# Probabilities scaled and turned by halves stream through the values, two query tiles at a time

## The chip, the cores and the metric

One core of one Trainium2 chip runs the program. The metric is device time in microseconds, the median of the runs of one kernel; lower is better. The engines are TensorE (PE, with its weight loads PEld), VectorE (DVE), ScalarE (ACT), GpSimd (POOL) and SyncE (SP, which issues DMAs).

## The reference

512 tokens of width 1024 pass a first block (a gated delta rule with its MLP) and then a second one, which mixes two kinds of attention. Only the second block's attention is touched:

```
q, k, v from h @ w_in_2        # 8 heads of width 64 over 2 groups of keys and values
p = masked_softmax(q k^T)      # two branches: selected keys and window; causal here
o = gate * (p @ v)             # summed over three branches for each head (the third reads blocks of keys)
o_mla = softmax(q' k'^T) @ v'  # 8 more heads, keys and values made from a latent
y = concat(o, o_mla) * silu(z) @ w_out_2
```

All is in float32, and the output must be close to a float32 reference.

## The kernel before, in words

Activations and weights of the large products are split into two parts, a rounded one and the rest (`hhi`, `hlo`, `whi`, `wlo`, type fp32r), and each product is made of three fp32r products: hi with hi, lo with hi, hi with lo (L2272). A small product is a plain float32 matmul, which the trace shows as two instructions of TensorE.

The attention of the second block is a spine of 96 steps, `for i in range(N_STEPS + 3)`, written out in the same order on every engine. Steps 0 to 63 are the sixteen pairs of head and branch of the two groups ("nsa"), steps 64 to 95 the 8 latent heads ("mla"); four steps are one head, one for each query tile of 128 tokens, and step i has (i % 4 + 1) * 128 keys. A step's work goes through the engines like this, with its line in the profile:

- PE `scores` (L3037): one float32 product into one of two PSUM banks.
- DVE `most`: the causal mask is added in PSUM (L2060), the row maximum is taken (L2062) and negated (L2064).
- ACT `soft` (L1138): the exponential into `prob`, with its row sum; two buffers.
- PE `turned`, two steps later (L3045): i % 4 + 1 transposes of `prob` into PSUM bank 4.
- ACT `turned` (L1146): the copy of bank 4 into `probT`, two buffers.
- PE `values`, three steps later (L3059): for each key tile `probT` is the weight (128x128) and `v`, 64 columns, moves. The output is tokens by 64.
- DVE `weigh` (L2070, L2076): the reciprocal of the row sum, times the gate. DVE `combine` (L2093, L2097): the output is scaled by it and added into `o_nsa` or written into `o_mla`, tokens by head width.

Between these PE runs six (five in three of four steps from 32 to 63, none in 68 to 71) of the 512-column products of the projections (`fill`), so that PE always has work. Other jobs sit at fixed steps (`jobs(i)` on each engine): rotations, the third branch's windows and softmax (steps 9 to 44), latent projections (54 to 85). On ACT `spine_units(i)` runs first in a step. At 16 steps (4, 8, ... 32, 37, 41, 46, 51, 55, 60, 64, 68) it copies the finished unit out of PSUM and splits the next weights into `whi` (L1050); POOL then makes `wlo` (L1358). At the end of the nsa steps PE turns `o_nsa` back (`turn_mixed`, L2887, steps 69 and 70), DVE multiplies it with the gate `zs2` (`mix`, L2033), ACT and POOL split it, and the output projection can start (step 72). `o_mla` is turned at steps 75, 83 and 91 and at the end (L3068).

The order on each engine is that of the code; semaphores count finished steps. On DVE a step is `most(i)`, `weigh(i-1)`, `combine(i-3)`, `jobs(i)`.

## Time and profile before

| | |
|---|---|
| three runs, median | 1089.87 us (1088.97 to 1091.43) |
| the profiled execution | 1092.04 us, span 1090.2 us |
| granted TensorE clock | 0.995 of full speed |
| PE busy | 1064.6 us, 98% |
| DVE, ACT, POOL busy | 56%, 43%, 44% |
| attention spine | from 751.4 us to about 1070 us of the span |

A line of the page names the source line, the engine, the operation, output and inputs, how many there were, the busy time and the mean of one, and then how long the engine stood idle before them and who released it. In the timeline the first two columns are start and duration. Matmul durations overlap: the distance from one start to the next is what one costs.

### The profile page before, as it was taken

Reading aid. Unit: us, or ns where it says so; the run is one execution under the profiler, and the core shown is the slowest. Engines: PE = TensorE matmul, PEld = TensorE weight load, DVE = VectorE, ACT = ScalarE, POOL = GpSimd, SP = SyncE. Lnnn points to the kernel's source line nnn. Section 1 sums busy time; section 2 is a strip of 40 time slices with the busy share of each in tenths; the row PEclk is TensorE's granted clock in tenths of the full one; section 3 lists DMA queues with packets and bytes.
Section 4 is the critical chain, followed back from the end, with each engine's and each line's share of the span. In section 5 each row is a group of like instructions: output and inputs, shape, how many; then the busy total and the mean of one; then the engine's idle time right before and its main releaser. Section 6 shows DMA issues by size and latency. Waiting matters only on the chain. (4 is left out here: it accounts for less than half of the span.)

```text
span 1090.2 us, 16275 instructions
## 1 busy us (share of the span) xinstructions
PE 1064.6 (98%) x5659; PEld 878.4 (81%) x5659; DVE 611.7 (56%) x1365; ACT 473.7 (43%) x1057; POOL 483.9 (44%) x276
## 2 busy tenths in 40 slices
PE   7999999999999999999999999999999999999997
PEld 6888888888878888888888888877788887766775
DVE  6777747767646646512122126436956767644677
ACT  6654346566543431531331333343334444454544
POOL 5786413332436775774574575346222122113230
PEclk9999999999999999999999999999999999999999
DMA  6554431221106154354343543514112011000011
GB/s 214 145 136 130 109 97 49 78 58 50 56 25 209 49 174 156 96 174 135 116 154 102 149 154 97 150 27 110 40 39 68 21 39 49 20 20 11 20 69 78
DMA packets 167157, 100.08 MB, mean 92 GB/s; under 512 B 30424, under 2 KB 160812, under 8 KB 166060
## 3 DMA queue, kind: packets, MB, share of 16 engines
q1 hardware_dynamic: 166924, 99.06, 31.3%
q8 instruction: 43, 0.70, 0.3%
q14 instruction: 30, 0.25, 0.1%
q10 hardware_dynamic: 160, 0.07, 0.0%
HBM read 95.69 MB, written 3.16 MB: 91 GB/s over the span
## 5 line engine op out<-in xcount | busy, mean ns | idle before, releaser
L1260 POOL TENSOR_TENSOR wlo<-stage,whi 128x1024 fp32r<-128x1024 f32 (+1 forms) x105 | 274.5, 2618 | 215.8 <-ACT whi L763 215.4
L2272 PE MATMUL ps<-hhi,whi 128*128 128x512 f32 (+1 forms) x728 | 306.9, 422 | 1.9 <-DVE gated L2033 0.9
L2272 PE MATMUL ps<-hhi,wlo 128*128 128x512 f32 (+1 forms) x728 | 296.7, 408 | 0.0
L2272 PE MATMUL ps<-hlo,whi 128*128 128x512 f32 (+1 forms) x728 | 288.5, 400 | 0.0
L2272 PEld LDWEIGHTS ps<-hhi,whi 128*128 128x128 f32 (+1 forms) x728 | 137.0, 188 | 36.1 <-issue 5.4
L1358 POOL TENSOR_TENSOR wlo<-stage,whi 128x1024 fp32r<-128x1024 f32 (+3 forms) x40 | 73.3, 1835 | 205.5 <-ACT whi L1050 205.5
L763 ACT ACTIVATE whi<-stage 128x1024 fp32r<-128x1024 f32 x104 | 109.7, 1056 | 120.7 <-PE ps L2272 88.8
L2272 PEld LDWEIGHTS ps<-hhi,wlo 128*128 128x128 f32 (+1 forms) x728 | 137.2, 188 | 30.1 <-issue 6.6
L2272 PEld LDWEIGHTS ps<-hlo,whi 128*128 128x128 f32 (+1 forms) x728 | 137.1, 188 | 26.2 <-issue 1.9
L2272 PE MATMUL ps<-ahi,whi 128*128 128x512 f32 x312 | 124.1, 398 | 3.4 <-POOL alo L1310 3.4
L1138 ACT ACTIVATE prob<-ps,aneg 128x128 f32<-128x128 f32 (+1 forms) x96 | 50.7, 528 | 168.8 <-DVE aneg L2064 122.9
L2272 PE MATMUL ps<-alo,whi 128*128 128x512 f32 x312 | 122.2, 392 | 0.0
L2272 PE MATMUL ps<-ahi,wlo 128*128 128x512 f32 x312 | 122.2, 392 | 0.0
L1790 DVE TENSOR_TENSOR hf<-relu 128x512 f32<-128x512 f32 x32 | 27.8, 867 | 112.1 <-ACT relu L1026 108.4
L1796 DVE TENSOR_TENSOR xT<-xT,ps 128x512 f32<-128x512 f32 x32 | 22.0, 688 | 102.7 <-PE ps L2272 102.7
L2272 PEld LDWEIGHTS ps<-ahi,whi 128*128 128x128 f32 x312 | 58.7, 188 | 15.0 <-POOL alo L1310 3.9
L2272 PEld LDWEIGHTS ps<-alo,whi 128*128 128x128 f32 x312 | 58.6, 188 | 11.8
L2272 PEld LDWEIGHTS ps<-ahi,wlo 128*128 128x128 f32 x312 | 58.7, 188 | 10.9
L1485 DVE SCALAR_TENSOR_TENSOR acc<-ps,convw,acc 128x511 f32<-128x511 f32 (+2 forms) x72 | 53.6, 745 | 10.2 <-ACT acc L796 8.6
L1026 ACT ACTIVATE relu<-ps 128x512 f32<-128x512 f32 x32 | 19.1, 598 | 92.4 <-PE ps L2272 92.4
L3059 PEld LDWEIGHTS ps<-v,probT 128*128 128x128 f32 x320 | 45.6, 191 | 4.4
L1340 POOL TENSOR_TENSOR alo<-hf,ahi 128x512 fp32r<-128x512 f32 x32 | 45.3, 1416 | 8.5 <-ACT ahi L1020 8.5
(399 smaller groups left out, 1765.2 us busy)
## 6 DMA issues: line engine op xcount, KB each, us to landing
stage<-dn_w_in SPq DMA_DIRECT2D x32, 512.0 KB, 4.2
stage<-mlp_w_up SPq DMA_DIRECT2D x32, 512.0 KB, 4.6
stage<-mlp_w_down SPq DMA_DIRECT2D x32, 512.0 KB, 4.6
mod_w<-ada_w SPq DMA_DIRECT2D x8, 1536.0 KB, 6.6
stage<-w_in SPq DMA_DIRECT2D x17, 512.0 KB, 3.6
gcrow<-gc_rows SPq DMA_DIRECT2D x16, 256.0 KB, 3.7
stage<-dn_w_out SPq DMA_DIRECT2D x8, 512.0 KB, 3.4
stage<-w_in SPq DMA_DIRECT2D x9, 256.0 KB, 3.0
```

The costliest lines, as they stand in the source:

```text
L763: act.activation(whi[:, slot, 0:ks, 0:cols], stage[:, slot, 0:ks, 0:cols], ACT.Copy).then_inc(s["w_hi"], 1)
L1026: act.activation(relu[:, m % 2], up_bank(q, m), ACT.Relu).then_inc(s["mlp_relu"], 1)
L1138: act.activation(prob[:, i % 2, 0:keys], ps[:, 2 + i % 2, 0:keys], ACT.Exp, scale=SCALE if kind == "nsa" else SCALE_M, bias=aneg[:, i % 2: ...
L1260: pool.tensor_tensor(wlo[:, slot, 0:ks, 0:cols], stage[:, slot, 0:ks, 0:cols], whi[:, slot, 0:ks, 0:cols], ALU.subtract).then_inc(s["w_lo" ...
L1340: pool.tensor_tensor(alo[0][:, m], af[:, m % 2], ahi[0][:, m], ALU.subtract).then_inc(s["mlp_lo"], 1)
L1358: pool.tensor_tensor(wlo[:, n % RING, 0:ks, 0:cols], stage[:, n % RING, 0:ks, 0:cols], whi[:, n % RING, 0:ks, 0:cols], ALU.subtract).then_ ...
L1485: dve.scalar_tensor_tensor(out=a[:, t:T], in0=u[:, 0:T - t], scalar=convw[:, (3 - t) * 3 + seq, h:h + 1], in1=a[:, t:T], op0=ALU.mult, op1 ...
L1790: dve.tensor_tensor(af[:, m % 2], relu[:, m % 2], relu[:, m % 2], ALU.mult).then_inc(s["mlp_f"], 1)
L1796: dve.tensor_tensor(xT[:, m], xT[:, m], ps[:, (U_MLP + m) % 2, :], ALU.add).then_inc(s["res"], 1)
L2272: mm = pe.matmul(bank, w[:, slot, k - ks[0], 0:width], x[:, k], start=(i == 0), stop=(i == len(todo) - 1))
L3059: mm = pe.matmul(ps[:, value_bank(i), 0:DK], probT[:, i % 2, c * P:(c + 1) * P], v, start=(c == 0), stop=(c == qt))
```

## The change

`prob` is scaled before it is turned. ACT multiplies the reciprocal with the gate (`scaled`, one column) and then `prob` with the result, in place, one step after the exponential. PE turns it as before. ACT copies the turned block into an fp32r tile (the high part, `hi_even` or `probT`), and DVE writes the difference between PSUM and that copy into a second one (`turned_low`, the low part). The values are held as weights: 64 columns of high part and 64 of low part side by side (`vst`, `v_mla`). `values(p)` now runs once for two query tiles, at even steps: for each key tile that both need one product of 256 moving columns, and one of 128 columns for the last key tile, first for the high part of the probabilities, then for the low part. The output has 128 partitions (64 for each half of the values) and lies turned: head width by tokens. For nsa, both branches and all four tiles of a head add up in bank 7, and DVE adds the two halves to `o_nsa` once in eight steps; for mla it combines each pair. The turns of the mixed outputs go away. The third branch's values and the latent values are made in the layout that this needs; the latent values come in eight jobs (steps 63 to 66 and 78 to 81) instead of four. DVE now starts a step with `weigh(i-1)` and `turned_low(i-3)`, ahead of `most(i)`. Two bfloat16 constants that nothing read are gone.

```diff
         def step_key(i):
             if i < N_NSA:
-                return "nsa", i // 16, i // 8 % 2, i // 4 % 2, i % 4
+                return "nsa", i // 16, i // 4 % 2, i // 8 % 2, i % 4
...
+            def scaled(i):
+                kind, e, b, g, qt = step_key(i)
+                keys, coef = (qt + 1) * P, ainv[:, i % 4:i % 4 + 1]
+                act.wait_ge(s["at_inv"], i + 1)
+                if kind == "nsa":
...
+                    act.activation(coef, ainv[:, i % 4:i % 4 + 1], ACT.Copy, scale=gate2[:, qt, at:at + 1]).then_inc(s["at_coef"], 1)
+                    act.wait_ge(s["at_coef"], i + 1)
+                act.activation(prob[:, i % 2, 0:keys], prob[:, i % 2, 0:keys], ACT.Copy, scale=coef).then_inc(s["at_scale"], 1)
+
             def turned(i):
-                keys = (i % 4 + 1) * P
                 act.wait_ge(s["at_t"], i + 1)
-                if i >= 2:
-                    act.wait_ge(s["at_o"], i - 1)
-                act.activation(probT[:, i % 2, 0:keys], ps[:, 4, 0:keys], ACT.Copy).then_inc(s["at_tev"], 1)
+                if i >= 4:
+                    act.wait_ge(s["at_o"], i // 2 - 1)
+                act.activation(turned_tile(0, i), ps[:, 4, 0:(i % 4 + 1) * P], ACT.Copy).then_inc(s["at_tev"], 1)
...
             for i in range(N_STEPS + 2):
                 if i < N_STEPS:
                     spine_units(i)
+                if 1 <= i <= N_STEPS:
+                    scaled(i - 1)
+                if i < N_STEPS:
                     soft(i)
...
-            turned_rows(0, "vs")
             rotated("ks", kz[0], None)
+            value_low(0, "vs")
...
-            def mix(k, bank):
-                after(dve, "pe", f"turned {k}")
+            def mix(k):
+                dve.wait_ge(s["at_done"], combined(N_NSA // 2 - 1 if k < 4 else N_NSA // 2 + 4 * (k - 3) - 1))
                 if k >= 2:
                     after(dve, "pool", f"mix low {k - 2}")
-                done(dve.scalar_tensor_tensor(out=gated[:, k % 2], in0=bank, scalar=0.5, in1=zs2[:, k],
+                done(dve.scalar_tensor_tensor(out=gated[:, k % 2], in0=out_tile(k), scalar=0.5, in1=zs2[:, k],
...
+            def turned_low(i):
+                dve.wait_ge(s["at_tev"], i + 1)
+                dve.tensor_tensor(turned_tile(1, i), ps[:, 4, 0:(i % 4 + 1) * P], turned_tile(0, i), ALU.subtract).then_inc(s["at_lo"], 1)
+
+            def combine(p):
+                kind, e, b, g, x = pair_key(p)
+                if kind == "nsa" and p % 4 < 3:
+                    return
+                n, bank = combined(p), ps[:, 7, :] if kind == "nsa" else pair_cols(x)
+                dve.wait_ge(s["at_o"], p + 1)
...
             for i in range(N_STEPS + 3):
+                if 1 <= i <= N_STEPS:
+                    weigh(i - 1)
+                if i >= 3:
+                    turned_low(i - 3)
                 if i < N_STEPS:
                     most(i)
...
-                if 1 <= i <= N_STEPS:
-                    weigh(i - 1)
+                if 5 <= i and i % 2:
+                    combine((i - 5) // 2)
...
             def turned(i):
                 qt = i % 4
-                pe.wait_ge(s["at_exp"], i + 1)
+                pe.wait_ge(s["at_scale"], i + 1)
                 if i:
-                    pe.wait_ge(s["at_tev"], i)
+                    pe.wait_ge(s["at_lo"], i)
...
-            def values(i):
...
+            def values(p):
+                kind, e, b, g, x = pair_key(p)
+                opens, shuts = kind == "mla" or (x, b) == (0, 0), kind == "mla" or (x, b) == (1, 1)
+                n, bank = 2 * x + 1, pair_cols(x)
+                pe.wait_ge(s["at_lo"], 2 * p + 2)
...
+                for part in range(2):
+                    t = turned_at(part, p)
+                    both = t[:, 0:2 * n * P].rearrange("p (j c i) -> p j c i", j=2, c=n)
+                    for c in range(n):
+                        pe.matmul(bank.rearrange("p (j i) -> p j i", j=2), v_tile(p, c), both[:, :, c, :],
+                                  start=opens and part == 0 and c == 0, stop=False)
+                    mm = pe.matmul(bank[:, P:2 * P], v_tile(p, n), t[:, 2 * n * P:(2 * n + 1) * P], start=False, stop=shuts and part == 1)
...
-                if i >= 3:
-                    values(i - 3)
+                if i >= 4 and i % 2 == 0:
+                    values(i // 2 - 2)
```

PE before, at step 23 (`kz` are keys, `v` values, `const,prob` a transpose, the rows with `hhi` and `hlo` fillers; an fp32 product is one row here):

```order
L3037 MATMUL ps<-kz_112,q2T 128x512
L2272 MATMUL ps<-hhi,whi 128x512
L2272 MATMUL ps<-hhi,wlo 128x512
L2272 MATMUL ps<-hlo,whi 128x512
L2272 MATMUL ps<-hhi,whi 128x512
L3045 MATMUL ps<-const,prob 128x128 x2
L2272 MATMUL ps<-hhi,wlo 128x512
L2272 MATMUL ps<-hlo,whi 128x512
L3059 MATMUL ps<-v_0_113,probT 128x64
```

PE after the change, from the transpose of step 22 to the scores of step 23:

```order
L3100 MATMUL ps<-const,prob 128x128
L2346 MATMUL ps<-hhi,wlo 128x512
L2346 MATMUL ps<-hlo,whi 128x512
L3120 MATMUL ps<-probT,vst_113 128x256 x3
L3122 MATMUL ps<-probT,vst_113 128x128
L3120 MATMUL ps<-lo_odd_165,vst_113 128x256 x3
L3122 MATMUL ps<-lo_odd_165,vst_113 128x128
L3092 MATMUL ps<-kz_140,q2T 128x512
```

The products with the values stand at every second step, eight (or four) in a row, and none at the steps between; each is a wide one with the values as weight.

ACT before, around the hook of step 24 (`cn<-ps` and `whi<-stage` are the hook):

```order
L1138 ACTIVATE prob,asum<-ps,aneg 128x512
L1146 ACTIVATE probT<-ps 128x256
L1101 ACTIVATE cn<-ps 128x512
L1050 ACTIVATE whi<-stage 128x1024
L1138 ACTIVATE prob,asum<-ps,aneg 128x128
```

ACT after the change, at the same place:

```order
L1188 ACTIVATE prob,asum<-ps,aneg 128x512
L1208 ACTIVATE hi_even_162<-ps 128x256
L1144 ACTIVATE cn<-ps 128x512
L1093 ACTIVATE whi<-stage 128x1024
L1200 ACTIVATE acoef<-ainv,gate_125 128x1
L1202 ACTIVATE prob<-prob,acoef 128x512
L1188 ACTIVATE prob,asum<-ps,aneg 128x128
```

Between the hook and the next exponential stand two new instructions.

DVE before, steps 26 and 27:

```order
L2064 TENSOR_SCALAR aneg<-amax 128x1
L2070 RECIPROCAL ainv<-asum 128x1
L2076 TENSOR_TENSOR acoef<-ainv,gate_128 128x1
L2093 SCALAR_TENSOR_TENSOR o_nsa<-ps,acoef,o_nsa 128x64
L2060 TENSOR_TENSOR ps<-ps,const_119 128x128
```

DVE after the change, steps 26 to 28 (`lo_even` is the low part; the two rows with `o_nsa` are `combine`):

```order
L2147 TENSOR_TENSOR lo_even_164<-ps,hi_even_162 128x128
L2133 TENSOR_TENSOR ps<-ps,const_118 128x128
L2135 TENSOR_REDUCE amax<-ps 128x1
L2137 TENSOR_SCALAR aneg<-amax 128x1
L2159 TENSOR_TENSOR o_nsa<-o_nsa,ps 64x512
L2163 TENSOR_TENSOR o_nsa<-o_nsa,ps 64x512
L2053 SCALAR_TENSOR_TENSOR csc<-ps,const_118 128x128 x4
L2143 RECIPROCAL ainv<-asum 128x1
L2147 TENSOR_TENSOR lo_even_164<-ps,hi_even_162 128x256
```

The low part now stands ahead of the mask and maximum of the next step, and behind all jobs of the step before.

## Rows read from the trace of the kernel before

**Rows 1.** Page, part 1: busy time and share of the span.

```profile
PE 1064.6 (98%) x5659; PEld 878.4 (81%) x5659; DVE 611.7 (56%) x1365; ACT 473.7 (43%) x1057; POOL 483.9 (44%) x276
```

**Rows 2.** Windows, steps 88 to 91: length, busy of engines, clock, DMA share, GB/s.

```profile
1038.60:1050.10 11.50, 11.50 (x69) 9.49 (x68) 7.87 (x24) 5.08 (x17) 2.95 (x4) 1.00 0.43 150
```

**Rows 3.** Lines by form, PE, products with the values: busy us, mean ns.

```profile
L3059 PE MATMUL ps<-v,probT 128*128 128x64 f32 x320 | 42.5, 263 | 0.0
L3059 PE MATMUL ps<-v_mla,probT 128*128 128x64 f32 x160 | 21.2, 264 | 0.0
```

**Rows 4.** Timeline of PE, end of step 26: start, duration.

```profile
838.75 1.00 PE L3059 MATMUL ps<-v,probT 128*128 128x64 f32 x8
839.59 1.08 PE L3037 MATMUL ps<-kz,q2T 128*128 128x512 f32 x2
```

**Rows 5.** Timeline of PE, last products: fp32r products of 256 columns.

```profile
1074.45 0.28 PE L3099 MATMUL ps<-hlo,whi 128*128 128x256 f32 x1
1074.57 0.38 PE L3110 MATMUL ps<-const,xT 128*128 128x128 f32 x2
```

**Rows 6.** Timeline of PE, step 91: the turn of a mixed output.

```profile
1048.77 0.60 PE L2887 MATMUL ps<-const,o_mla 128*128 128x128 f32 x4
1049.20 0.38 PE L3045 MATMUL ps<-const,prob 128*128 128x128 f32 x2
```

**Rows 7.** Timeline of DVE and ACT, step 26: from the mask to the copy.

```profile
837.46 0.30 DVE L2060 TENSOR_TENSOR ps<-ps,const 128x128 f32<-128x128 f32 x1 [0.41 <-PE ps L3037]
837.79 0.56 DVE L2062 TENSOR_REDUCE amax<-ps 128x1 f32<-128x384 f32 x1
838.39 0.15 DVE L2064 TENSOR_SCALAR aneg<-amax 128x1 f32<-128x1 f32 x1
838.57 0.58 ACT L1138 ACTIVATE prob<-ps,aneg 128x384 f32<-128x384 f32 x1 [1.78 <-DVE aneg L2064]
839.15 0.27 ACT L1146 ACTIVATE probT<-ps 128x128 f32<-128x128 f32 x1
```

**Rows 8.** Lines by form, ACT, 750 to 1062 us: exponential and copy, widest and narrowest.

```profile
L1138 ACT ACTIVATE prob<-ps,aneg 128x512 f32<-128x512 f32 x24 | 16.5, 688 | 61.5 <-DVE aneg L2064 49.4 <-PE ps L3045 8.4 <-issue 3.7
L1146 ACT ACTIVATE probT<-ps 128x512 f32<-128x512 f32 x23 | 13.5, 588 | 0.0
L1138 ACT ACTIVATE prob<-ps,aneg 128x128 f32<-128x128 f32 x24 | 8.8, 369 | 23.0 <-DVE aneg L2064 11.9 <-issue 11.0
L1146 ACT ACTIVATE probT<-ps 128x128 f32<-128x128 f32 x24 | 6.4, 268 | 0.0
```

**Rows 9.** Lines by form, DVE, same stretch: PSUM with SBUF into SBUF.

```profile
L2016 DVE TENSOR_TENSOR o_nsa<-o_nsa,ps 128x512 f32<-128x512 f32 x4 | 2.8, 688 | 0.4
```

**Rows 10.** Lines by form, ACT, same stretch: a copy of SBUF, and the hook's split.

```profile
L1158 ACT ACTIVATE hhi<-gated 128x512 fp32r<-128x512 f32 x7 | 4.2, 631 | 0.1
L1050 ACT ACTIVATE whi<-stage 128x1024 fp32r<-128x1024 f32 x15 | 16.0, 1064 | 0.0
```

**Rows 11.** Timeline, DVE and PE ahead of the spine.

```profile
735.21 5.60 DVE L1906 TENSOR_TENSOR kz<-rcos,rsin 64x512 f32<-64x512 f32 x2
740.14 0.42 PE L2760 MATMUL ps<-const,raw 24*128 24x24 f32 x4
```

**Rows 12.** Timeline of DVE, step 32.

```profile
859.86 1.63 DVE L1992 TENSOR_TENSOR csc<-csc,csm 128x1024 f32<-128x1024 f32 x1
```

**Rows 13.** Timeline, POOL and DVE at step 46, PE at step 48.

```profile
904.27 2.36 POOL L1358 TENSOR_TENSOR wlo<-stage,whi 128x1024 fp32r<-128x1024 f32 x1 [14.42 <-ACT whi L1050]
904.33 2.31 DVE L2076 TENSOR_TENSOR acoef<-ainv,gate 128x1 f32<-128x1 f32 x1
909.78 0.52 PE L3045 MATMUL ps<-const,prob 128*128 128x128 f32 x3 [0.92 <-ACT probT L1146]
```

**Rows 14.** Timeline, DVE and PE at steps 70 to 72.

```profile
983.55 0.69 DVE L2033 SCALAR_TENSOR_TENSOR gated<-ps,zs 128x512 f32<-128x512 f32 x1 [0.55 <-POOL hlo L1410]
984.35 0.47 PE L2272 MATMUL ps<-hhi,whi 128*128 128x512 f32 x1 [0.89 <-DVE gated L2033]
```

More of the change, by code:

```diff
@@ L270, in build @@
         kz = [sb("kz0", [P, 2, T]), None]
-        v2 = [sb(f"v2_{b}", [P, CH, P]) for b in range(2)]
+        vst = [sb("vst0", [P, 2, CH, P], F32R), None]
         cn = sb("cn", [P, 3, T])
@@ L423, in build @@
                 "block out 0", "z 1", "block out 1", "block out 2", "block out 3", "z 2", "z 3", "z 4", "sin up 0",
[10 rows of a table removed]
[3 rows of a table added]
+                "sum oA3", "latent low 5", "latent low 6", "sum oA4", "latent low 7", "q ready 7", "mixed 5",
[7 rows of a table added]
             "pool": ["mlp low 1", "mlp low 3", "mlp low 5", "mlp low 7", "zero", "norm low 1", "norm low 3",
@@ L1101, in taken, with value_high @@
                 done(act.activation(dst, src, ACT.Copy), f"ev {name}")
+            def value_high(b, name):
+                after(act, "pe", f"turn {name}")
+                done(act.activation(vst[b][:, :, :, 0:DK], aux_bank(f"turn {name}").rearrange("p (c g d) -> p g c d", c=CH, g=2), ACT.Copy),
+                     f"{name} high")
             taken("vs")
@@ new lines, in combine, with latent_low @@
+                dve.wait_ge(s["at_part"], n)
+                dve.tensor_tensor(head_rows(p), head_rows(p), bank[DK:2 * DK], ALU.add).then_inc(s["at_done"], 1)
+            def latent_low(n):
+                after(dve, "act", f"latent values {n}")
+                v = v_mla[n // 4][:, n % 4]
+                done(dve.tensor_tensor(v[:, :, DK:2 * DK], aux_bank(f"latent values {n}")[:, 0:4 * DK].rearrange("p (h d) -> p h d", h=4),
+                                       v[:, :, 0:DK], ALU.subtract), f"latent low {n}")
@@ L3012, in jobs @@
                     project_k(PAIR_STEP.index(i - 1))
-                if i in (69, 70):
-                    pe.wait_ge(s["at_done"], N_NSA)
-                    for k in range((i - 69) * 2, (i - 69) * 2 + 2):
-                        after(pe, "dve", "z 7" if k < 2 else f"mixed {k - 2}")
-                        turn_mixed(k, ps[:, k % 2, :])
-                if i in (75, 83, 91):
-                    turn_mla(4 + (75, 83, 91).index(i))
             def scores(i):
```

219 lines of the change are left out of this document (113 added, 106 removed), and 52 rows, old and new, of tables (JOBS, STEPS).

## The prediction

> **What bounds the kernel now.** First the page's busy shares: PE 98%, DVE 56%, ACT and POOL 44% [rows 1]. PE has nearly no idle time over the whole span, so a product taken from it shortens the kernel as long as the others keep up. Next a window over four undisturbed steps of the spine (88 to 91): it is 11.50 us long, PE is busy for 11.50, and the granted clock is 1.00 [rows 2]. In it PE turns one mixed output, at 0.43 [rows 6], so four plain steps are 11.07, or 2.77 each. After PE and its weight loads the row gives DVE 7.87, ACT 5.08 and POOL 2.95 [rows 2]: DVE has some 30% to give. Then the lines by form, which count what is to go, and the timelines of one step, which give the chain that the others must run through per step. They matter because the change takes work from PE and puts some of it on DVE and ACT, in series with what they do for each step.
>
> **What PE saves.** A head has four steps with 1+2+3+4 = 10 key tiles. Before, each is two rows of 64 columns, 20 in all; the 480 rows of the trace are 24 heads of 20 [rows 3]. Eight stand 0.84 apart from the next product, 0.105 each [rows 4] (their durations of 263 ns overlap; the distance counts). So 2.10 a head. After: the pair of tiles 0 and 1 has one wide and one narrow product, the pair 2 and 3 three wide and one narrow, both for high and low part: 12. The one fp32r product of 256 columns that the trace shows takes 0.12 to the next [rows 5]. The narrow one (fp32r, 128 columns moving) isn't in the trace: no less than 0.105, what 64 columns took; as a bound above I take twice that, 0.21, the two rows of a float32 product of 64 columns, and for a worse case 0.33. I choose 0.12, since a product of half the columns beside it should not be dearer. 12 x 0.12 = 1.44; saved 0.66 a head, 24 heads: 15.8. The eight turns of mixed outputs go, 8 x 0.43 = 3.4 [rows 6]. At step 46 the gate product of one column took DVE 2.31 while POOL made `wlo` in 2.36, and PE waited 0.92 for what followed [rows 13]; that operation now is ACT's: 0.9. Sum of gains 20.1. The values of the third branch and the latent values cost PE the same as before and only stand elsewhere.
>
> In the Trainium skill, page "SBUF — State Buffer", section "Who interferes with whom", a VectorE instruction with two SBUF inputs and a GpSimd instruction that reads SBUF lock each other out, whoever is second waiting for the whole of the first. The trace agrees as far as it goes: 2.31 for one column beside 2.36 of POOL. By that rule the change wins here (the operation leaves DVE) and loses at the mix, whose first input moves from PSUM to SBUF; without it, with each mix at its 0.69, the sum below would be 2.4 less.
>
> **What the others must do now.** Before, DVE's share of a step (mask, maximum, negation) waited for scores only. Now `turned_low(i-3)` stands ahead of `most(i)` on DVE, it needs ACT's copy, the copy stands behind ACT's exponential of a later step, and that one needs `most`. This is a ring: most, exponential, copy, low part, most of the next step. At 384 keys: start of the mask to start of the exponential 1.11, exponential 0.58 [rows 7]. Scaled to the mean of 320 keys (0.13 for 128 columns in the maximum, estimated from 688 ns for 512 [rows 9] less 0.15 for one column [rows 7]) 1.04; exponential 0.53 and copy 0.43 as means of widest and narrowest [rows 8]; low part, one input in PSUM, 0.69 at 512 columns [rows 9], so 0.49 at the mean; handover from the negation to the exponential 0.03 [rows 7], the same from the copy to the low part. Sum 2.53 a step, 10.1 for four. PE now wants 11.07 - 0.66 = 10.4 where six fillers stand in a step, and about 9.75 where three of four steps have five (a 512-column filler about 0.22, twice the 256-column one and less). So the ring is hidden by 0.3 in four steps, or sticks out by 0.35. That is the heart of the forecast. ACT's scaling (631 ns for 512 columns of SBUF [rows 10]) stands between the ring's instructions and mostly falls into ACT's wait for DVE: 49.4 us ahead of the 24 widest exponentials, 11.9 ahead of the 24 narrowest [rows 8], so 2.1 and 0.5 us a step; only in the narrow steps can it come out.
>
> **The 16 hooks.** There ACT first copies out of PSUM (0.6) and splits `whi` (1.06 [rows 10]); then come the new column (about 0.2) and the scaling (up to 0.63), all ahead of the exponential: 2.5, where DVE's low part and maximum, in parallel, take 1.3. The ring is late by up to 1.2 at a hook. PE turns a step's probabilities two steps behind its scores, so some of this is absorbed: bounds 0 and 1.2.
>
> **Losses, by place.**
> - Start: `post vs` moves behind `post ks`, which takes 5.60 from 735.21 and so ends at 740.81 [rows 11]. With 0.69 for the new low part PE's turn of the gate can start at 741.6 instead of 740.14: 1.4, and 0.3 for what stands behind: 1.7.
> - Steps 4 to 21, where DVE also has rotations, normalisation and windows: five hooks at 0.6 (half of the 1.2), and two combines of 2 x 0.69 [rows 9] in front of a low part, 0.9 of each uncovered: 4.8. Bounds 0 and 10.
> - Step 32: the operation of 1.63 on DVE [rows 12] now stands ahead of a low part that PE waits for: 1.6.
> - Steps 22 to 63: the ring, 8 heads x 0.35 = 2.8; nine hooks at 0.18 = 1.6. Sum 4.4, bounds 0 and 2.8 + 9 x 1.2 = 14.
> - Steps 68 to 72: no fillers, so PE waits for the others already (0.89 at 984.35, behind DVE's mix, which waited 0.55 for POOL [rows 14]). The mix reads two SBUF tiles after the change, while POOL makes the low part of the mix before: 1.2 for each of two, taken as half of the 2.31 of [rows 13] (bounds 0 and 2.31). A low part and a maximum stand behind mixes 3 and 4: 1.6. PE's saving isn't worth anything here: 0.8. Sum 4.8.
> - Steps 73 to 95: ring under PE by 0.3 in four steps, but sums of partial outputs (0.69 [rows 9]) are ahead of the low parts: 23 steps at 0.09 = 2.0.
> - End: the last low part waits behind a sum (0.69), is 0.69 itself, and the last values take 0.3 more than before: 1.7.
>
> Losses 1.7 + 4.8 + 1.6 + 4.4 + 4.8 + 2.0 + 1.7 = 21.0. Net 21.0 - 20.1 = +0.9. The profiled execution was 1092.04 (span 1090.2), so 1092.9 in such an execution; the median of the runs is 2.2 below the profiled one, so 1090.8, say **1091**.
>
> **Rivals.**
> (B) The waits are hidden and PE stays the bound. For it: DVE is only 56% and ACT 44% busy [rows 1], ring and PE are level, and a queue of two steps takes up the hooks. Against it: the instructions of the ring are in series, so busy shares say little. Only the places without cover remain: start 1.7, steps 68 to 72 4.8, end 1.7. 1092.0 - 20.1 + 8.2 = 1080.1, less 2.2: **1078** (1073 if most of the 4.8 is hidden too).
> (C) The ring decides at the hooks, and the kernel gets slower. Place: the hook on ACT; price: 1.2 at each of the eleven from step 24 to 68, in place of the 1.6 counted; it decides as soon as PE's lead over the ring is under 1.2 when the hook comes, which a ring of the same length as PE's work can't build up again. 0.9 + 13.2 - 1.6 = 12.5: 1104.5, less 2.2: **1102**. For it: ring 10.1 beside 10.4 and 9.75. Against it: before, PE was 98% busy [rows 1] with 1.7 us of hook on ACT at the same steps, so the queue of two steps can hide that much.
> (D) The narrow product isn't cheap. 24 x 4 = 96 of them; at 0.21 that is 8.6 more, at 0.33 20, and 1099 to 1111 come out, unless the ring hides it. For it: the trace shows no such product. Against it: 0.12 for 256 columns.
> (E) The change doesn't do what it says on PE: a product with 256 moving columns in a strided, paired view costs more than the plain one. No row speaks for it; it is part of (D).
>
> **Numbers.** Forecast band (A, 1086 to 1096) 0.40; B 0.30; C 0.24; D 0.06. The range: 1074 to 1105, which leaves out a tenth below (B better than its sum) and under a tenth above (C with hooks before step 24 at the full price, D at 0.33). A measurement of this kernel tells apart about 0.2%, 2.2 us: 1087.7 to 1092.1 is "same". Of A I give 0.12 to faster, 0.16 to same, 0.12 to slower; with B 0.30 and C and D 0.30: faster 0.42, same 0.16, slower 0.42. The forecast alone has 1086 to 1096.
>
> **What would show each step.** The saving: eight products with the values, from their first start to the next instruction, 0.96; at over 1.2 D is right. PE's busy time should fall by about 19. The ring: PE idle before its transposes with DVE's low part as releaser, some 20 us in all, in steps 22 to 63 about 4; nearly none there speaks for B, 12 or more for C, and then single gaps of a us stand right behind the hooks on ACT. The start: turn of the gate 1.4 later. Steps 68 to 72: mixes over 1.2 long beside POOL's low part; if all take 0.69, POOL doesn't hold them and 2.4 come back. The end: last values behind the last low part. The forecast is wrong if PE stays 97% busy or more (B), or if the granted clock falls in the spine because of PE's gaps, which before, at 98%, was 1.00 [rows 2].

## The result and the profile after

| | before | after |
|---|---|---|
| median of 6 runs each | 1091.37 us (1088.97 to 1091.88) | 1097.47 us (1095.89 to 1098.52) |
| ratio | | 1.0056, 95% interval 1.0046 to 1.0067 |
| profiled execution, span | 1090.2 us | 1095.9 us |

The kernel became slower by 6 us. The forecast was 1091 and the range 1074 to 1105; the time fell between the forecast band (1086 to 1096) and the rival that ended on the slow side (1102). The direction had been left open (0.42 to 0.42).

Part of the 6 us is TensorE's clock. The record has the mean granted clock of every execution. The six of the kernel after had 0.990 to 0.993, the executions of the kernel before that ran beside the experiments 0.992 to 0.998. At 0.993 the kernel after took 1095.9 and 1096.4 us (two executions) and the kernel before 1092.6 to 1093.6 (seven): about 3 us at the same clock. The other half goes with a lower clock of the kernel after.

The page's busy shares of the kernel after, to be read against [rows 1]:

```profile
PE 1050.4 (96%) x5435; PEld 854.3 (78%) x5435; DVE 639.4 (58%) x1355; ACT 541.7 (49%) x1223; POOL 483.5 (44%) x276
```

PE has 14.2 us less work than before (1064.6 to 1050.4) and yet the span is 5.7 us longer: PE stands idle for some 20 us more. ACT has 68 us more work, DVE 28, and both are still far from full.

First the part that came as forecast. The windows of one head of the spine in which PE never waits (columns as in [rows 2]); the same steps 84 to 87, from the scores of 84 to those of 88, of before

```profile
1024.96:1038.58 13.62, 13.62 (x70) 10.15 (x70) 7.01 (x23) 7.21 (x20) 2.75 (x3) 1.00 0.07 20
```

and of after:

```profile
1026.26:1039.20 12.94, 12.94 (x62) 9.21 (x60) 9.67 (x28) 9.31 (x24) 2.78 (x3) 1.00 0.07 21
```

Four steps went from 13.62 to 12.94, 0.68 less, at a clock of 1.00 in both (forecast: 0.66). Steps 16 to 19, without waits too, went from 16.03 to 15.38, 0.65 less. PE is busy all through, while DVE grew from 7.01 to 9.67 and ACT from 7.21 to 9.31. The timeline of PE at step 95 gives the price of the new products (start, duration):

```profile
1059.38 0.51 PE L3120 MATMUL ps<-probT,v_mla 128*128 128x256 f32 x3
...
1059.73 0.22 PE L3122 MATMUL ps<-probT,v_mla 128*128 128x128 f32 x1
...
1059.79 0.56 PE L3120 MATMUL ps<-lo_odd,v_mla 128*128 128x256 f32 x3
...
1060.19 0.22 PE L3122 MATMUL ps<-lo_odd,v_mla 128*128 128x128 f32 x1
...
1060.26 1.07 PE L3092 MATMUL ps<-km,q2T 128*128 128x512 f32 x2
```

Eight products with the values take 0.88 from the first start to the scores behind them (forecast 0.96): three wide ones 0.35 and 0.40, so 0.12 to 0.13 each, and a narrow one 0.06 and 0.07. The product of 128 moving columns, for which 0.12 had been taken and 0.21 and 0.33 held open, costs about half of a wide one, and rival D is out.

Then where PE waits. The view of waits of PE, 750 to 1062 us of the kernel after (us in total, times, longest):

```profile
PE ps L3100 <- DVE lo_odd L2147: 9.5, 11, 2.3
PE ps L3100 <- DVE lo_even L2147: 9.0, 15, 2.0
```

The same view of the kernel before:

```profile
PE ps L2868 <- ACT zth L1191: 1.6, 1, 1.6
PE ps L3045 <- ACT probT L1146: 1.4, 2, 0.9
```

26 waits, 18.5 us, all at the transposes and all ended by DVE's low part of the step ahead (forecast: some 20). In steps 22 to 63 they are 7.2 us, where about 4 had been put. Three waits are 2.0 to 2.3 us long (steps 20, 33 and 69). Behind the first and the third the clock fell, behind the second it did not. The windows round the first (the third column from the end is the clock):

```profile
823.00:824.00 1.00, 0.75 (x5) 0.74 (x6) 0.92 (x5) 0.86 (x2) 1.00 (x1) 1.00 0.00 0
824.00:828.00 4.00, 4.00 (x13) 3.16 (x13) 2.52 (x7) 1.40 (x5) 0.82 (x1) 0.57 0.48 131
828.00:829.00 1.00, 1.00 (x7) 0.68 (x6) 0.41 (x1) 0.00 (x0) 0.00 (x0) 1.00 0.00 0
```

From 824 to 828 the granted clock is 0.57 of full, and 0.50 in the two microseconds from 825 to 827, the lower of its two levels (1.2 GHz). PE had stood idle for 2.00 us ending at 823.25. PE is fully busy in these four us and does in them what takes 2.3 at the upper level, so 1.7 us go on top of the gap. Before, the clock fell in the spine once, from 986.9 to 990.4, round the second of two gaps of 0.89 and 1.57 us at step 72. Now it falls at 824, and for 7 us (0.52 from 977.8 to 984.8) at steps 69 to 71. The falls take 5.1 us of work at full speed from the spine of the kernel after and 1.7 from that of before, so of the 5.7 us of span up to 3.4 are the clock. Ahead of the spine both executions lost time to the clock as well (after at 165 and 295, before at 707), and at 719 the two are level again.

What is to be read at that first gap is the queue on DVE (timeline at steps 19 and 20):

```profile
820.23 0.38 ACT L1208 ACTIVATE hi_even<-ps 128x256 fp32r<-128x256 f32 x1
...
820.44 1.84 DVE L2033 TENSOR_SCALAR vbd<-ps 32x64 f32<-32x64 f32 x8
...
822.31 0.26 DVE L2036 TENSOR_TENSOR ktmp<-ktmp,table 128x62 f32<-128x62 f32 x1
...
822.50 0.15 DVE L2143 RECIPROCAL ainv<-asum 128x1 f32<-128x1 f32 x1
822.68 0.42 DVE L2147 TENSOR_TENSOR lo_even<-ps,hi_even 128x256 fp32r<-128x256 f32 x1
...
823.25 0.52 PE L3100 MATMUL ps<-const,prob 128*128 128x128 f32 x3 [2.00 <-DVE lo_even L2147]
```

ACT's copy was done at 820.61, and the low part made from it started at 822.68: eight copies of block values (1.84) stood in front. Before, these transposes waited for ACT's exponential and ACT's last copy. DVE stood in that path only with the maximum that the exponential needs.

The gaps at steps 33 and 92 are of the same kind. At step 33 a subtraction with two SBUF inputs stands ahead of the low part, beside POOL's `wlo`, and takes 2.63 where it took 1.63 before [rows 12]. At step 92 it is the mix of a mixed output, 1.13 beside POOL, and PE waits 1.50:

```profile
862.57 2.38 POOL L1428 TENSOR_TENSOR wlo<-stage,whi 128x1024 fp32r<-128x1024 f32 x1 [10.41 <-ACT whi L1093]
...
863.39 2.63 DVE L2061 TENSOR_TENSOR csc<-csc,csm 128x1024 f32<-128x1024 f32 x1
...
866.71 0.52 PE L3100 MATMUL ps<-const,prob 128*128 128x128 f32 x3 [2.25 <-DVE lo_odd L2147]
...
1051.68 1.13 DVE L2106 SCALAR_TENSOR_TENSOR gated<-o_mla,zs 128x512 f32<-128x512 f32 x1
```

The distance of the two kernels at the start of a step's scores, put together from the two timelines. What PE saved is put at 0.65 for a head and 0.43 for a turn [rows 6]; the other 1.4 are gaps of before at steps 36 and 48, and 1.3 is an estimate for work of the latent values that moved to steps 78 to 81. Lost is the change of distance plus what was saved, and it holds the time at the lower clock too:

| place | distance at its end | saved | lost | forecast of the loss |
|---|---|---|---|---|
| up to step 0 | +1.4 | 0 | 1.4 | 1.7 |
| steps 0 to 19 | +1.4 | 3.3 | 3.3 | 4.8 |
| 20 to 34 | +6.6 | 2.4 | 7.6 | 1.6 and a third of 4.4 |
| 35 to 66 | +0.9 | 5.2 + 1.4 + 1.3 | 2.2 | two thirds of 4.4 |
| 67 to 72 | +1.5 | 1.0 + 1.7 | 3.3 | 4.8 |
| 73 to 91 | +0.2 | 3.1 + 1.3 - 1.3 | 1.8 | 2.0 |
| 92 to 94 | +1.9 | 0.5 | 2.2 | 0 |
| 95 to the end | +5.7 | 0.6 | 4.4 | 1.7 |

What was saved comes to 20.5 (forecast 20.1), the losses to 26.2 (forecast 21.0). Three places hold 14 of them: steps 20 to 34, step 92, and the end.

The end, DVE and PE of the kernel after:

```profile
1070.35 0.60 ACT L1208 ACTIVATE probT<-ps 128x512 fp32r<-128x512 f32 x1 [3.26 <-PE ps L3100]
...
1072.05 1.45 DVE L2123 SCALAR_TENSOR_TENSOR xT<-ps,mod,xT 128x512 f32<-128x512 f32 x2
...
1073.41 0.41 DVE L2245 TENSOR_TENSOR hlo<-gated,hhi 128x256 fp32r<-128x256 f32 x1
...
1073.75 0.68 DVE L2147 TENSOR_TENSOR lo_odd<-ps,probT 128x512 fp32r<-128x512 f32 x1
...
1074.48 0.62 PE L3120 MATMUL ps<-probT,v_mla 128*128 128x256 f32 x3 [1.78 <-DVE lo_odd L2147]
```

The copy of the last turned block was done at 1070.95, its low part started at 1073.75, behind sums, a mix and the mix's low part; PE stood for 1.78 us.

### The profile page after: what moved, and what is told of

Its sections match the earlier page's. It is cut to its first block, busy times and chain, and to the rows that moved or that the text cites. A ratio compares the mean times of both kernels' runs of the same rounds, so it can differ in the third digit from the quotient of the medians.

```text
span 1095.9 us, 15801 instructions
## 1 busy us (share of the span) xinstructions
PE 1050.4 (96%) x5435; PEld 854.3 (78%) x5435; DVE 639.4 (58%) x1355; ACT 541.7 (49%) x1223; POOL 483.5 (44%) x276
## 4 chain that ended last, share of the span: by engine, by line
PE 77%; DVE 12%; issue 4%; ACT 4%; POOL 2%; DMA 1%; SPq 0%; DVEq 0%; ACTq 0%; POOLq 0%
PE ps L2346 55%; PE ps L3092 3%; PE ps L3100 2%; PE ps L3120 2%; DVE amax L2135 1%; DVE lo_odd L2147 1%; PE ps L2607 1%; PE ps L2843 1%; PE ps L2947 1%; PE ps L2627 1%; DVE ps L2133 1%; PE ps L2618 1%; DVE ps L1528 1%; PE ps L2531 1%; DVE blocks L1642 1%
## 5 line engine op out<-in xcount | busy, mean ns | idle before, releaser
L3100 PEld LDWEIGHTS ps<-const,prob 128*128 128x128 f32 x240 | 29.6, 143 | 46.8 <-issue 36.7
L3100 PE MATMUL ps<-const,prob 128*128 128x128 f32 x240 | 43.5, 279 | 18.7 <-DVE lo_odd L2147 9.5
```

The costliest lines, as they stand in the source:

```text
L3100: mm = pe.transpose(ps[:, 4, c * P:(c + 1) * P], prob[:, i % 2, c * P:(c + 1) * P], ident)
```

## The experiments

Theory Q (queue): the gain is lost at single places where longer DVE work stands ahead of a low part that PE waits for, and the clock falls behind some of these gaps. Theory R (ring): the chain mask, exponential, copy, low part is too long for a step everywhere. Theory H (hooks): ACT's hooks with the new instructions ahead of the exponential make it late. Each ratio is to the kernel before on the same chip; the change itself has 1.0056 (1.0046 to 1.0067).

**1. The end.**

```diff
@@ DVE, i == N_STEPS
+                        if m == 2:
+                            turned_low(N_STEPS - 2)
                         last_sum("C", m)
@@ DVE, i == N_STEPS + 1
                     last_sum("C", 4)
+                    turned_low(N_STEPS - 1)
                     last_sum("C", 5)
```

> The changed kernel, with the low part of step 94 ahead of the sums of C2 and C3 on DVE, and that of step 95 ahead of the sum of C5 and of the mix. Theory Q (the gain is lost where other DVE work stands ahead of a low part that PE waits for): the 1.78 us of PE ahead of the last values and part of the waits before go, 2 to 3 us faster than the changed kernel, 1094.5 to 1095.5. Rival R (the chain mask, exponential, copy, low part as such is too long for a step, wherever it stands): the sums only change places with the low parts, within 0.7 us of 1097.5.

Measured: 1095.04 us, ratio 1.0034 (1.0020 to 1.0048), so 2.4 us less than the change by the ratios. The gap ahead of the last values is gone from the waits. The edit itself is worth about 1.0 us, though: in the two traces this kernel is 0.8 ahead of the change already at the scores of step 0, where the programs are the same, and still 0.8 at step 95; at the end it is 1.8. Six of its seven executions had a clock of 0.993, four of the six of the change 0.990 or 0.991. The direction is as Q says, the size is less than the 2 to 3 expected.

**2. Step 19, the low part alone.**

```diff
                 if i == 19:
+                    turned_low(17)
                     block_keys()
```

> The changed kernel, with the low part of step 17 ahead of the 1.8 us of block value copies on DVE (step 19) instead of behind them. Theory Q with the clock as a second price: PE's gap of 2.00 us at step 20 goes, and with it the four us at a granted clock of 0.5 that follow it (another 1.7 us): 3 to 3.7 us less, about 1094. If the fall of the clock has another cause than the gap: 2 us less at most, 1095.5. Rival R: nothing, since the chain behind is as long as before.

Measured: 1100.85 us, ratio 1.0087 (1.0071 to 1.0103): 3.4 us slower than the change, the wrong way for either theory. The timeline of this kernel:

```profile
819.85 1.84 DVE L2033 TENSOR_SCALAR vbd<-ps 32x64 f32<-32x64 f32 x8
...
821.16 2.37 POOL L1428 TENSOR_TENSOR wlo<-stage,whi 128x1024 fp32r<-128x1024 f32 x1
...
821.73 1.93 DVE L2036 TENSOR_TENSOR ktmp<-ktmp,table 128x62 f32<-128x62 f32 x1
...
823.59 0.15 DVE L2143 RECIPROCAL ainv<-asum 128x1 f32<-128x1 f32 x1
...
824.09 0.72 ACT L1202 ACTIVATE prob<-prob,acoef 128x512 f32<-128x512 f32 x1
...
826.28 0.73 PE L3103 MATMUL ps<-const,prob 128*128 128x128 f32 x4 [2.32 <-ACT prob L1202]
```

The gap at step 20 is gone, but now the reciprocal of step 19 stands behind the same work, ACT scales with it, and everything behind it is late: PE waits 2.32 us one step on, and the clock is at 0.50 from 827 to 830. In the row with 1.93 a new thing is seen: a product of 62 columns with both inputs in SBUF, that took 0.26 in the kernel after, ends 0.13 us behind POOL's 2.37. In the kernel after it had started 0.09 us ahead of POOL's instruction. In the trace of this run the move loses 0.7 us against the change from step 20 to step 23, and up to step 95 the distance then stays within 0.2. The profiled execution took 1097.03 at a mean clock of 0.993, and the five others 1099.5 to 1101.8 at 0.985 to 0.989: the rest of the 3.4 us goes with a lower clock, at places that no trace shows.

**3. Step 19, reciprocal and low part.**

```diff
                 if i == 19:
+                    weigh(19)
+                    turned_low(17)
                     block_keys()
```

> The changed kernel with both things that PE waits for through DVE, the reciprocal of step 19 and the low part of step 17, ahead of the block value copies of step 19. In the run that moved the low part alone, the gap of 2.0 us went and one of 2.3 us stood two steps later, released by ACT's scaling, which had waited for the reciprocal behind the same copies. Theory Q: with both moved neither gap is there and the clock stays at 1.0: 3 to 3.7 us less than the changed kernel, about 1094. Rival R: the gap moves again to the next item of the chain and the time stays at 1097 or above.

Measured: 1097.35 us, ratio 1.0063 (1.0042 to 1.0084), no change. The gap moved again, to 2.13 us at step 21, where the mask of step 20 stood behind the locked-out product (1.92). At this place the wording of rival R came true, though the cause isn't the ring's length, as the next run shows.

**4. The same, with one SBUF input.**

```diff
+                done(dve.scalar_tensor_tensor(out=ktmp[:, 1, :, 0:NC], in0=bank[:, 0:2 * NCP].rearrange("p (g n) -> p g n", g=2)[:, :, 0:NC],
+                                              scalar=0.5, in1=at_blocks(1), op0=ALU.mult, op1=ALU.mult), "kc cos")
                 after(dve, "pool", "block zero")
...
-                after(dve, "dve", "kc")
-                done(dve.tensor_tensor(ktmp[:, 1, :, 0:NC], ktmp[:, 0, :, 0:NC], at_blocks(1), ALU.mult), "kc cos")
```

> As the run with reciprocal and low part moved ahead at step 19, and with the product of the block keys with the cosine (62 columns) made from PSUM with one SBUF input, ahead of the copies, in place of two SBUF inputs behind them. In that run this product took 1.92 us beside POOL's low part of the weights (2.38), and a gap of 2.13 us with a fall of the clock stood behind it. If the lock-out by POOL is what holds DVE there, the product takes under 0.3 us and the gap at step 21 shrinks to under 0.5, with no fall of the clock near 826: 3 to 4 us less than the changed kernel, 1093 to 1095 (before at 1091.4). Rival: DVE is full there, the gap stays above 1.5.

```profile
820.15 0.25 DVE L2029 SCALAR_TENSOR_TENSOR ktmp<-ps,table 128x62 f32<-128x62 f32 x1
820.21 1.28 POOL L1453 TENSOR_TENSOR rcos<-raw,table 128x512 f32<-128x512 f32 x1 [10.86 <-ACT raw L1144]
...
821.44 2.38 POOL L1428 TENSOR_TENSOR wlo<-stage,whi 128x1024 fp32r<-128x1024 f32 x1
...
822.19 0.30 DVE L2133 TENSOR_TENSOR ps<-ps,const 128x128 f32<-128x128 f32 x1
...
822.92 0.25 DVE L2040 TENSOR_TENSOR ktmp<-ps,table 128x62 f32<-128x62 f32 x1
...
824.87 0.63 PE L3104 MATMUL ps<-const,prob 128*128 128x128 f32 x4 [0.61 <-DVE lo_odd L2147]
```

Measured: the product takes 0.25, the mask starts at 822.19 (1.8 earlier than in run 3), the gap is 0.61, and step 22 starts 1.9 and step 23 2.7 us earlier: 1.9 of gap and delay, 0.8 of clock. That the long product was what held DVE is shown. The edit changes two things, its inputs and its place, and at the new place it starts 0.06 us ahead of POOL's instruction, so this row alone doesn't tell them apart. The last DVE row does: a product of 62 columns with one input in PSUM starts 1.5 us into POOL's `wlo` and takes 0.25. The time: 1095.50 us, ratio 1.0040 (1.0024 to 1.0056); 1.7 to 2.5 us better than the change and run 3, but the intervals overlap. At nearly the same clock the runs part: three executions of this kernel at 0.992 took 1094.2 to 1094.5, three of run 3 at 0.993 took 1097.0 to 1097.6.

This run shows something else too. Its profiled execution took 1099.71 us, the quickest one 1094.15. The windows, of this kernel

```profile
865.00:871.00 6.00, 6.00 (x22) 5.07 (x21) 5.13 (x13) 3.43 (x11) 0.00 (x0) 0.50 0.00 0
1053.00:1055.00 2.00, 2.00 (x8) 1.73 (x8) 0.88 (x3) 2.00 (x6) 0.92 (x1) 0.50 0.00 0
1077.00:1082.00 5.00, 4.81 (x22) 4.81 (x23) 3.71 (x9) 1.39 (x6) 0.00 (x0) 0.50 0.00 0
```

and of run 3:

```profile
865.00:871.00 6.00, 3.80 (x24) 3.25 (x24) 5.83 (x15) 3.91 (x9) 0.00 (x0) 1.00 0.01 3
1053.00:1055.00 2.00, 2.00 (x13) 1.83 (x14) 1.80 (x6) 1.55 (x6) 0.04 (x1) 1.00 0.00 0
1077.00:1082.00 5.00, 4.94 (x38) 4.24 (x37) 5.00 (x12) 2.94 (x13) 0.00 (x0) 1.00 0.00 0
```

Both have the same gaps of 2.24 us at step 33, 1.50 at step 92 and 1.78 at the end; in one execution the clock fell behind the first two and once more at the end, in the other at none of them. At steps 34 to 36 the fall costs 1.8 us, at 92 to 94 1.6. So gaps of about 2 us cost what they are long, and sometimes as much again. The unprofiled executions have no clock by stretches, but their mean clock is on record and the spread goes with it: this kernel took 1094.2 to 1094.5 at 0.992, 1096.6 and 1097.1 at 0.989, and 1099.7 at 0.987.

**5. ACT's scaling left out.**

```diff
-                act.activation(prob[:, i % 2, 0:keys], prob[:, i % 2, 0:keys], ACT.Copy, scale=coef).then_inc(s["at_scale"], 1)
@@ PE, turned
-                pe.wait_ge(s["at_scale"], i + 1)
+                pe.wait_ge(s["at_exp"], i + 1)
```

> The changed kernel without ACT's multiplication of the probabilities (PE turns them as they come from the exponential; the outputs are not weighted; the column of coefficients is still made on ACT). Theory Q: DVE holds the low parts up, so ACT's 0.4 to 0.7 us a step are hidden nearly everywhere, 0 to 2 us less, 1095.5 to 1097.5. Rival H (ACT's hooks with the two new instructions ahead of the exponential make the ring late): 5 to 10 us less, 1088 to 1092.

Measured: 1098.24 us, ratio 1.0065 (1.0045 to 1.0085): no difference to the change. 52 us of ACT's work are hidden. Q, against H as far as the scaling goes.

**6. ACT's hooks behind the exponential.**

```diff
-                if i < N_STEPS:
-                    spine_units(i)
                 if 1 <= i <= N_STEPS:
                     scaled(i - 1)
                 if i < N_STEPS:
                     soft(i)
+                    spine_units(i)
```

> The changed kernel with ACT's hook (copy out of PSUM and split of the next weights) behind the scaling and the exponential of its step instead of ahead of them. Rival H (the hooks make the ring late, up to 1.2 us each): 5 to 13 us less than the changed kernel. Theory Q (they are covered): within 2 us of it, 1095.5 to 1099.5; the copies come 1.5 us later and can hold PE's fillers or POOL's split.

Measured: 1109.64 us, ratio 1.0173 (1.0154 to 1.0191), 13 us slower. The spine's waits (750 to 1060) are 25.1 us where the change has 18.5. Behind the exponential the hook stands ahead of the copy of the turned block, and that copy is what DVE's low part needs. The hook ahead of the exponential was the cheaper place. That doesn't show that it costs nothing there; the trace of the change does: at the steps with a hook PE waits 0.54 us or less for a low part, 1.6 in all, but for step 20, where DVE's block values are the cause. H had up to 1.2 for each, and falls. That ACT's copy is on the path while its scaling isn't fits runs 5 and 6 together; the waits are only 6.6 us longer, though, with a span 9.5 longer, and where the rest goes is left open.

**7. The low part behind the maximum.**

```diff
+                if i < N_STEPS:
+                    most(i)
                 if i >= 3:
                     turned_low(i - 3)
-                if i < N_STEPS:
-                    most(i)
```

> The changed kernel with the low part behind the mask and the maximum of the step on DVE instead of ahead of them. Theory Q: each low part comes about 1 us later where PE has no slack (0.2 us waits before the transposes are already there in even steps), so the gaps add up, 10 to 40 us more, 1107 to 1137. Rival R (it is the order low part first that closes the ring and costs the time): faster than the changed kernel, 1085 to 1095.

Measured: 1140.83 us, ratio 1.0447 (1.0425 to 1.0468): 43 us slower than the change. The waits of PE for the low parts:

```profile
PE ps L3100 <- DVE lo_odd L2147: 29.2, 30, 2.6
PE ps L3100 <- DVE lo_even L2147: 20.9, 27, 2.7
```

57 waits and 50 us, where the change has 26 and 18.5. So the low part ahead of the mask isn't what costs the time: behind it, the loss against before grows from 6 to 49 us.

**8. The low part with one column.**

```diff
-                dve.tensor_tensor(turned_tile(1, i), ps[:, 4, 0:(i % 4 + 1) * P], turned_tile(0, i), ALU.subtract)
+                dve.tensor_tensor(turned_tile(1, i)[:, 0:1], ps[:, 4, 0:1], turned_tile(0, i)[:, 0:1], ALU.subtract)
@@ PE, values
-                    t = turned_at(part, p)
+                    t = turned_at(0, p)
```

> The changed kernel with a low part of one column in place of the whole block (both parts of the values products read the high part, so the low parts of the probabilities are left out of the result). DVE has 0.15 instead of 0.29 to 0.69 us a step, 0.35 less on the mean, 33 us of DVE work in all. Theory Q: the short waits of 0.2 at every second step go (some 4 us) and each gap behind other DVE work gets shorter by 0.3 to 0.5 (some 8 of them, 3 us): 5 to 9 us less than the changed kernel, 1088 to 1092. Rival R (ring decides everywhere): 15 us less or more.

Measured: 1084.52 us, ratio 0.9939 (0.9922 to 0.9957): 12.8 us less than the change, more than Q said and less than R. The waits:

```profile
PE ps L3100 <- DVE lo_odd L2147: 6.6, 5, 2.1
PE ps L3100 <- DVE lo_even L2147: 4.9, 6, 1.7
```

The fifteen short waits are gone, eleven stay, and these are the places with other work in front. So the length of the low parts themselves (29 us of DVE) costs 13 us of time, about half of what was lost. Most of that may be put to R; a small part is the long gaps of Q getting shorter (2.00 to 1.73 at step 20, 1.32 to 1.05 at step 52, 1.78 to 1.24 at the end). The other half stays without it, at the places of Q.

**9. High parts of the mixed outputs a step earlier.**

```diff
-                if i in (70, 71):
-                    for k in ((i - 70) * 2, (i - 70) * 2 + 1):
+                if i in (69, 71):
+                    for k in (i - 69, i - 68):
                         mix_high(k)
```

> The changed kernel with ACT's high parts of the mixed outputs 0 and 1 one step earlier (step 69 in place of 70). In the changed kernel they start at 982.7, 2.5 us after the mixes are done, POOL's low parts follow, and DVE stands for 2.8 us before mixes 2 and 3. If that chain sets steps 69 to 72, 2 to 3 us less than the changed kernel, 1094.5 to 1095.5. If the ring of the attention sets them (rival R), the earlier high parts only hold up the exponential: no gain, or 0.5 us more.

Measured: 1095.63 us, ratio 1.0051 (1.0031 to 1.0071): not told apart from the change. In the changed kernel the mixes look like this:

```profile
978.88 1.28 DVE L2106 SCALAR_TENSOR_TENSOR gated<-o_nsa,zs 128x512 f32<-128x512 f32 x2
...
980.26 0.69 DVE L2147 TENSOR_TENSOR lo_odd<-ps,probT 128x512 fp32r<-128x512 f32 x1
...
981.10 0.45 PE L3100 MATMUL ps<-const,prob 128*128 128x128 f32 x1 [1.44 <-DVE lo_odd L2147]
...
983.41 2.49 POOL L1480 TENSOR_TENSOR hlo<-gated,hhi 128x512 fp32r<-128x512 f32 x2 [6.68 <-ACT hhi L1220]
...
984.78 2.27 DVE L2106 SCALAR_TENSOR_TENSOR gated<-o_nsa,zs 128x512 f32<-128x512 f32 x2 [2.84 <-POOL hlo L1480]
```

Two mixes ahead of the reciprocal and the low part, PE stands 1.44 us for it; and mixes 2 and 3 take 2.27 beside POOL's low parts, where the first two take 1.28. That is 1.0 for both from the lock-out, where 2.4 had been put down. The earlier high parts go into ACT's free time, and in the trace of this run steps 71 and 72 together take 1.1 us less than in the change. The gaps at steps 69 and 70 are those of the low parts: 2.28 as before, and 2.36 where the change had 1.44.

**10 to 12. Versions with these orders put together.** The first has runs 1, 3 and 9, the pair of reciprocal and low part ahead of the long work also at steps 9, 32, 33 and 91, and the first values' low part ahead of the rotation of the keys.

```diff
-            rotated("ks", kz[0], None)
             value_low(0, "vs")
+            rotated("ks", kz[0], None)
@@ block_less_max
                 done(dve.tensor_reduce(csm[:, 0], block_rows, AX.X, ALU.max), "max")
+                weigh(32)
+                turned_low(30)
                 after(dve, "dve", "max")
```

> The changed kernel with five edits of order: low part of steps 94 and 95 ahead of the last sums; reciprocal and low part ahead of the long DVE work of steps 9, 19, 32, 33 and 91; high parts of mixes 0 and 1 a step earlier; the low part of the first values ahead of the rotation of the keys. Theory Q: 2.4 (end) + 3.5 (step 19) + 0.9 (9) + 2 (32, 33) + 1 (91) + 2 (mixes) + 1 (start) = about 12 less than the changed kernel, 1085 to 1088, faster than the kernel before. Rival R: each gap comes back at the next item, 1093 to 1095, as the end alone gives.

Measured: 1093.95 us, ratio 1.0029 (1.0017 to 1.0041): 3 us better than the change, a quarter of what Q had promised. In the trace step 0 starts 1.6 us earlier (versions with the same start as the change lie there up to 1.5 apart) and step 92 gives 1.1; step 20's gap moved to 21 as in run 3, step 10's to 11 (0.89 to 0.24 at the one, 0.46 to 1.07 at the other), and step 33's to 34 (2.25 to 0.43 at the one, 0.98 to 1.49 and another 0.47 for ACT's square at the other). Moving a gap's cause forward by one step brings the next item of the queue, so the pair must go ahead at each step in turn. The second has that, at steps 10, 27, 51, 69 and 70 as well, the product of run 4, and ACT's hook of step 68 last.

```diff
                     mix((i - 69) * 2)
+                    weigh(i)
+                    turned_low(i - 2)
                     mix((i - 69) * 2 + 1)
```

> The version with five edits of order, and besides: the same for steps 10, 27, 51 (ahead of the second half of a window, of the block scores, of the gate of z), 69 and 70 (between the two mixes); the cosine product from PSUM; ACT's hook of step 68 behind the copy of the turned probabilities. Gaps of the five-edit version that should go: 2.4 and 1 of clock at step 21, 0.8 at 11, 0.4 at 28, 1.1 at 52, 2 to 3 at steps 69 and 70; 7.5 to 8.5 in all, so 1085 to 1088 where before has 1091.4: faster than both. Rival R (the ring as such): only half of it comes, 1090.

Measured: 1090.09 us, ratio 0.9991 (0.9983 to 1.0000). Half of what was expected, 3.9 us of 8. At step 69 the gap stayed (2.55): the later hook let the gate of z wait for ACT's tanh for 2.0 us, ahead of the pair on DVE. The third puts the pair ahead of that too, and at step 5, has ACT square the latent before the exponential of the blocks, and ACT copy two halves at the end.

```diff
-                if i in (27, 51):
+                if i in (27, 51, 68):
                     weigh(i)
                     turned_low(i - 2)
```

> The version before this one (ten places with reciprocal and low part ahead) and besides: the same at step 5 (0.6) and at step 68 ahead of the gate of z, which then waited 2.0 us for ACT's tanh (1.1 and part of the clock behind it); on ACT at step 32 the square of the latent ahead of the exponential of the blocks (0.5); at the end ACT copies the first halves of the last two outputs in place of DVE (0.5 to 0.8). About 2.5 us less than the version before: 1087 to 1088.5, ratio to before 0.996 to 0.998, faster than both kernels. Rival R: no change, ratio 0.999.

Measured: 1089.22 us (1087.16 to 1090.54, 12 runs) against 1091.08 on the same chip, ratio 0.9982 (0.9972 to 0.9992): faster than both kernels, by 0.2% and 0.7%. At a clock of 0.993 it took 1087.9 and 1088.6, where the kernel before took 1092.6 to 1093.6. The expected 2.5 us were 1.0, and the intervals of the last two versions overlap. PE's waits for low parts in its spine are 11.6 us. The longest, 2.4 us, is at step 70, where PE has no fillers.

## Why the prediction was half right

- **PE's saving** held: 0.68 and 0.65 for four steps where 0.66 was worked out, 0.12 for a wide product as taken, 0.07 for a narrow one where 0.12 was. The view of busy time shows only 14 us less, where 19 had been put. Work at the lower clock counts as busy longer, and over the whole execution that adds 8.5 us to the kernel after and 3.4 to the kernel before, which makes up the other 5.
- **The balance** (20.1 saved, 21.0 lost) was the right way to put it: 20.5 and 26.2. The 5 us between the losses are most of the miss; another 1.5 is the base, since 2.2 had been taken off the profiled execution for a median of three executions, and the median of six is only 0.7 below it. That the time stayed in the range is in part luck: three places were put too low by 9.4 in sum, and the others too high by 4.2.
- **"Steps 22 to 63: the ring, 2.8, and nine hooks, 1.6"**: the ring is there, in its place and about its size. Steps 56 to 59, with five fillers, took 10.35 before and 10.46 after, where PE's own work is about 10.35 - 0.65 = 9.7 (forecast: 10.1 against 9.75), with waits of 0.36 and 0.21 for low parts. The hooks are not what makes it late: ACT's scaling costs nothing that can be told (run 5), the hook stands at its cheaper place, and the waits at the steps with a hook are short (run 6). The largest single wait from 35 to 66, 1.32 at step 52, is DVE's: a combine and the gate of z ahead of the low part.
- **"Step 32: 1.6"** and **"Steps 4 to 21: 4.8"** are the step that failed. They named the right kind of thing, DVE work ahead of a low part, but took the jobs by their length in the trace of before and did not go through the queue at each step. Step 19's block values (1.84) weren't in the sum, and step 32's subtraction took 2.63 beside POOL in place of 1.63. Together 7.6 at 20 to 34, where 3 were put. Step 92, where the mix stood in front, had no term at all and lost 2.2 with the two steps behind it.
- **The clock** was named only as what would make the forecast wrong, and by that sign it was: it fell behind two of the new gaps, and the sum has no term for it. At step 20 it cost 1.7 us. The 1.00 that the prediction gives for the spine of before was read in one window, steps 88 to 91; at step 72 the clock had fallen there too.
- **The end**: 1.7 was three items of one wait each; the last two low parts stood behind sums, a mix and its low part, 4.4, of which run 1 gave 1.0 back by the traces.
- **The lock-out by POOL**, weighed at two places, is there: the column of coefficients has left DVE, and PE's gap of 0.92 at step 48 is 0.42; at the mixes it was 1.0 and not 2.4; and it appeared where it hadn't been looked for, at 62 columns behind the block values (runs 3 and 4). The Trainium skill, page "SBUF — State Buffer", section "Who interferes with whom", has VectorE instructions with two SBUF inputs and GpSimd instructions that read SBUF lock each other out, and those with one SBUF input not. The traces of runs 3 and 4 agree on both halves, for 62 columns beside a `wlo` that was already running: 1.92 with two SBUF inputs, 0.25 with one.
- **The start**: 1.4 for the turn of the gate was 1.41 (741.55 against 740.14), and 1.40 reached step 0; the 0.3 more that had been put behind it did not come.
- **Rival C** ended on the right side by the wrong mechanism: not ACT's hooks but DVE's queue. **Rival B** was wrong: the waits weren't hidden.

## What to carry to other kernels

When an engine that had only late work gets an instruction that the bottleneck waits for, go through its queue step by step and write down what stands in front of that instruction; the sum of busy shares and the length of the chain both miss it. Put everything that the bottleneck will ask for (here reciprocal and low part, both) ahead of the long work, in consecutive steps, for a gap that is filled at one step comes back at the next item. And with a bottleneck at 98% busy, count a new gap of two us as up to four. When two versions differ by some us, compare executions at the same mean clock as well: here half of the difference was the clock.

## What the runs showed of the hardware

- A gap of TensorE of 2.24 us was followed by six us at a clock of 0.50 in one execution and by none in another, with the same instructions in the 20 us before it (run 4 and run 3; PE busy for 17.07 and 17.09 of them). The fall cost 1.8 us. Shorter gaps can be followed by one as well: in the kernel after the clock was at 0.50 behind gaps of 1.05 (165 us) and 1.47 (295 us), and the kernel before has the same two gaps and no fall. At 707 us of the kernel before it fell with PE busy for the whole 20 us ahead.
- The mean clock of an execution goes with its time: the kernel before took 1088.5 to 1090.8 us at 0.997 and 1092.6 to 1093.6 at 0.993.
- An fp32r product with 128 moving columns took 0.07 us to the next start, one with 256 moving columns 0.12 to 0.13 (0.40 for three), each with its own weight of 128x128; a float32 row of 64 columns had taken 0.105 [rows 4].
- A DVE product of 62 columns with two SBUF inputs took 1.93 us when it came behind the start of a POOL subtraction of 2.37 us (run 2), and 0.26 when it started 0.09 us ahead of one (kernel after). With one input in PSUM it took 0.25, started 1.5 us into such a subtraction (run 4).
